# A planner in place of a hand-written order: 256-query attention, crossbar transposes and gates beside attention in a diffusion-transformer step on eight cores

## What is computed

```python
h = rms_norm(x, norm1_w) * (1 + sc1) + sh1
q, k, v, u, g = split(h @ w_in)
q, k = rms_norm(q), rms_norm(k)              # latent tokens: 2-D rotary on q and k as well
s1, s2 = softmax(q1 @ k1.T / 8), softmax(q2 @ k2.T / 8)
att = rms_norm((s1 - lam * s2) @ v) * (1 - lam_init)
sgu = gelu(u) * (w_s @ layer_norm(gelu(g)) + b_s)   # w_s: 128x128 per group, in chunks of 128 tokens
x = x + g1 * (concat(att, sgu) @ w_o)
h = rms_norm(x, norm2_w) * (1 + sc2) + sh2
x = x + g2 * (square(relu(h @ w_ff1)) @ w_ff2)
```

## Time and profile before

| what | us |
|---|---|
| median of 3 runs (2780.09 to 2781.9) | 2781.86 |
| span of the profiled execution, slowest core | 2781.8 |
| spans of the eight cores | 2769.1 to 2781.8 |
| PE busy in the span | 2514.5 (90%) |
| DVE, ACT, POOL busy | 1286.9, 751.9, 100.3 |

### The profile page before, as it was taken

One profiled execution on the slowest core, in us unless ns is written; L12 is line 12 of the kernel. 1 busy time (PEld: TensorE's weight loads), 2 busy tenths in 40 slices (PEclk: granted clock), 3 DMA queues, 4 the chain that ended last, 5 costly groups with the idle time before them and its releaser, 6 DMA issues.

```text
span 2781.8 us, 39172 instructions; the slowest of 8 cores (2769.1 to 2781.8 us)
## 1 busy us (share of the span) xinstructions
PE 2514.5 (90%) x16144; PEld 1352.3 (49%) x16144; DVE 1286.9 (46%) x2471; ACT 751.9 (27%) x1699; POOL 100.3 (4%) x162
## 2 busy tenths in 40 slices
PE   1468799899889586999999999999999999999999
PEld 0356567666666243444444444444444444444444
DVE  0257363463563222344551735528264462835537
ACT  1145455555555463422231010010100101010010
POOL 0001100000000000000000000000000000000000
PEclk9679899999999777999999999999999999999999
DMA  9962433333422637055448232222322322322336
GB/s 181 184 176 90 65 73 65 65 72 72 70 59 57 109 67 131 12 99 170 156 139 213 48 59 46 51 55 46 56 51 46 60 47 46 61 46 47 59 76 182
DMA packets 58427, 237.15 MB, mean 85 GB/s; under 512 B 20176, under 2 KB 25872, under 8 KB 35216
## 3 DMA queue, kind: packets, MB, share of 16 engines
q0 software_dynamic: 22560, 150.25, 30.7%
q1 hardware_dynamic: 35696, 84.41, 9.4%
HBM read 352.34 MB, written 32.54 MB: 138 GB/s over the span
## 4 chain that ended last, share of the span: by engine, by line
PE 82%; DMA 7%; DVE 6%; ACT 3%; issue 1%; another core or an unknown queue 1%; POOL 0%; SPq 0%; DVEq 0%; ACTq 0%
PE ps L232 81%; PE ps L240 2%; DMA sel_t<-selsum 2%; DMA xt_129<-xs 1%; DMA wr_90<-wa 1%; DMA ada_120<-wa 1%; DMA attd<-on_117 1%; DMA kr_105<-ck 1%; DVE hT L262 1%; DVE hO L262 0%; DVE a_114 L257 0%; DVE o_115 L257 0%; ACT P_108 L250 0%; DVE t_102 L257 0%
## 5 line engine op out<-in xcount | busy, mean ns | idle before, releaser
L232 PE MATMUL ps<-hT,wf_13386 128*128 128x512 bf16 x1536 | 335.6, 380 | 0.0
L232 PE MATMUL ps<-wf_13385,aT 128*128 128x512 bf16 x1536 | 334.1, 379 | 0.0
L232 PE MATMUL ps<-hT,wf_13385 128*128 128x512 bf16 x1536 | 334.1, 379 | 0.0
L232 PE MATMUL ps<-wf_13386,aT 128*128 128x512 bf16 x1536 | 334.1, 379 | 0.0
L250 ACT ACTIVATE rl_14673<-ps 128x512 f32<-128x512 f32 x96 | 57.3, 597 | 855.7 <-PE ps L232 855.7
L232 PEld LDWEIGHTS ps<-hT,wf_13386 128*128 128x128 bf16 x1536 | 150.6, 98 | 182.2 <-issue 1.9
L232 PEld LDWEIGHTS ps<-hT,wf_13385 128*128 128x128 bf16 x1536 | 150.5, 98 | 181.0
L232 PEld LDWEIGHTS ps<-wf_13386,aT 128*128 128x128 bf16 x1536 | 150.5, 98 | 181.0
L232 PEld LDWEIGHTS ps<-wf_13385,aT 128*128 128x128 bf16 x1536 | 150.0, 98 | 181.5
L257 DVE TENSOR_TENSOR aT<-rl_14674 128x512 bf16<-128x512 f32 x96 | 66.5, 692 | 264.8 <-ACT rl_14674 L250 264.8
L257 DVE TENSOR_TENSOR aT<-rl_14673 128x512 bf16<-128x512 f32 x96 | 66.5, 692 | 262.5 <-ACT rl_14673 L250 262.4
(11 more groups left out here) (663 smaller groups left out, 2898.8 us busy)
## 6 DMA issues: line engine op xcount, KB each, us to landing
wr_90<-wa POOLq DMA_DIRECT2D x32, 1024.0 KB, 8.9
wf_13386<-wf POOLq DMA_DIRECT2D x32, 1024.0 KB, 8.6
wf_13385<-wf POOLq DMA_DIRECT2D x32, 1024.0 KB, 8.7
acc<-x1d SPq DMA_DIRECT2D x12, 1024.0 KB, 42.5
ys<-acc SPq DMA_DIRECT2D x32, 256.0 KB, 2.8
ada_120<-wa POOLq DMA_DIRECT2D x3, 2048.0 KB, 28.5
ada_121<-wa POOLq DMA_DIRECT2D x3, 2048.0 KB, 38.8
wr_89<-wqkv POOLq DMA_DIRECT2D x6, 1024.0 KB, 9.6
```

Of the source, the lines that this page charges most:

```text
L232: ins = e.matmul(o, lhsT=l, rhs=r, start=st, stop=sp, skip_group_check=True)
```

## The change

The generators and the clock `S.t` go. Each piece of work is now a thread that yields the events, buffers or banks that it needs; a discrete-event model of the five engines and of two DMA rings, with a booked cost for every operation, runs all threads at planning time, and an operation is put into the program when the model's engine takes it, by the priority of its thread. What is computed stays. The other parts of the change:

- Attention works on 256 queries throughout. Four key tiles make one burst of eight score matmuls into banks 0 to 3 (two for each map), and one exponential for each map reads 1024 columns from two banks. One token stands for the score banks and one for the output banks 4 and 5; banks 6 and 7 are left to all other work.
- The transposes of Q, K, the cached keys, the attention output (on its way back from DRAM) and the second norm are transfers through the DMA crossbar, issued from SP (`turn`). The 20 input tiles are still transposed on PE; for the last 14 the modulation now reads PSUM.
- The gate matmuls run in the attention phase 3, unactivated, into SBUF; GELU and norm follow after that phase. The 32 units of `wa1` follow one another from the end of the phase-0 projections. The gate's norm weight moves into the addition after the mixing.
- The order of the projections is K, V, Q; the third weight and the tiles 6 and 7 are loaded behind the eight modulation units, the other tiles once the last of these has landed.

The core of the diff:

```diff
+PE_SWITCH = 100.0
+DMA_RATE = 335.0
+DMA_LAT = 1900.0
...
+    def dispatch(self, eng):
+        if self.busy[eng] or not self.q[eng]:
+            return
+        _, _, ev, cost, emit, lat, mode, nbytes = heapq.heappop(self.q[eng])
...
+        if mode is not None and mode != self.mode:
+            cost += PE_SWITCH
+            self.mode = mode
+        emit()
...
+    def cact(self, n, aps=0, accum=False):
+        return 100 + 0.833 * n + 93 * aps + (190 if accum else 0)
...
+    def turn(self, out, in_, key, sbuf_src=True, dr=(), prio=None):
+
+        n = count(out)
+        return self.post("sp", 300.0 + 1.7 * n, lambda: self.add(
+            "sp", lambda e: e.dma_start_transpose(out=out, in_=in_), reads=[in_] if sbuf_src else [], writes=[out], key=key, dr=dr),
+            0, nbytes=n * 256 * 2, prio=prio)
...
+        for k2 in range(8):
+            j = yield banks
+            op = S.tr([(bank16(j)[:, (c * n + i) * 128:(c * n + i + 1) * 128], xn[xnbuf[t0 + i]][:, (2 * k2 + c) * 128:(2 * k2 + c + 1) * 128])
+                       for c in range(2) for i in range(n)], identb)
+            ends.append(S.spawn(out(j, k2, op), 19))
...
-        def s5(kr):
-            j = pg.take()
-            pt = pb(j)
...
+        dst = QT[s] if kind == "q" else KT[s]
+        yield S.turn(dst[:, t0:t0 + 2].rearrange("p t h n -> p (t h) n"), kr[kj], "kr%d" % kj)
+        krs.give(kj)
...
     def attention(p):
...
+        yield (banks, range(6))
...
+        for i0 in range(0, len(items), 4):
+            its = items[i0:i0 + 4]
+            yield [KTev[p][it[2] // 2] for it in its] + [QTev[p][it[1] // 256] for it in its]
+            pj = yield Ps
+            yield Stok
...
+                    ops.append((PS[:, m * 1024 + j * 256:m * 1024 + (j + 1) * 256], KT[s][r, kt, hh, :],
+                                QT[s][r, q0 // 128:q0 // 128 + 2, hh, :], True, True))
+            yield S.mm(ops, mode="row", cost=len(its) * 112.0)
+            es = [S.act(Pt[pj][:, m, 0:n], PS[:, m * 1024:m * 1024 + n], AF.Exp, scale=0.125) for m in range(2)]
...
+    def gates():
+        yield hO_end
+        for i in range(2):
+            link(S.load(flat(wg_t[i]), wg[i], "wg%d" % i, cast=True), wg_ev[i])
+        yield [proj_end[3], att_end[2], ada_end] + wg_ev
...
+                for k0 in range(0, 16, 4):
+                    op = S.mm([(bank(j), hts(kc, tt), wg_t[nb][:, kc, :], kc == 0, kc == 15) for kc in range(k0, k0 + 4)])
+                ends.append(S.spawn(out(j, tt, nb, op), 24))
...
+    def g_norm():
+        yield [att_end[3]]
+        yield S.table(GELU_SET)
...
+            link(S.turn(att_t[j], attd[tt].rearrange("p h d -> p (h d)"), "at%d" % j, sbuf_src=False, dr=[("att", tt, h) for h in range(8)]), at_ev[tt])
...
+        yield S.turn(h2T[:, :, tt * 128:(tt + 1) * 128], xm[j], "xm%d" % j)
...
+    for p in range(1, 4):
+        S.spawn(proj(p), 30)
+    for p in range(4):
+        S.spawn(attention(p), 10)
+    S.spawn(gates(), 32)
```

More of the change, by code:

```diff
@@ L230, in fn, with run, pick, is_ps @@
+    def run(self):
+        while self.heap:
+            t, _, f = heapq.heappop(self.heap)
+            self.now = t
+            f()
+        assert self.live == 0, "threads that wait for ever: %d" % self.live
+    def pick(self, costs):
+        return min(costs, key=lambda e: max(self.until[e], self.now) + self.backlog[e] + costs[e])
+    def is_ps(self, ap):
+        return self.tens[ap.tensor.name][0] == "p"
+    def mm(self, ops, mode="full", cost=None, prio=None):
         def fn(e):
@@ new lines, in acts, with emit @@
+    def acts(self, ops, cost, table=()):
+        def emit():
+            if table:
+                self.nc.scalar.preload_act_table_set(table[0])
+            for out, in_, func, bias, scale in ops:
+                rd = [in_] + [x for x in (bias, scale) if not isinstance(x, float)]
+                self.add("act", lambda e: e.activation(out=out, in_=in_, func=func, bias=bias, scale=scale), reads=rd, writes=[out])
+            if table:
+                self.nc.scalar.preload_act_table_set(table[1])
+        return self.post("act", cost, emit, LAT["act"])
@@ L292, in wait_all_stores, with count @@
                 self.nc.sync.wait_ge(self.sems[nd.sem], nd.val)
[L295 to L319 removed]
+def count(ap):
+    return int(np.prod([n for _, n in ap.ap[1:]]))
 def bview(ap, dims):
@@ L375, in build_program, with bank, bank16 @@
     S = Sched(nc)
-    ps = [S.psum("ps%d" % j, j) for j in range(8)]
-    def pb(j):
-        return ps[j].bitcast(BF16)
+    PS = S.psum("ps")
+    PSB = PS.bitcast(BF16)
+    banks = Pool(S, range(8))
+    def bank(j):
+        return PS[:, j * 512:(j + 1) * 512]
+    def bank16(j):
+        return PSB[:, j * 1024:(j + 1) * 1024]
     o = [0]
@@ L545, in ada_cols, with evs, link, rsqrt @@
-    def ada_cols(mod, bank, n, ch, k0, which):
+    def evs(n):
+        return [Ev() for _ in range(n)]
+    def link(op, ev):
+        op.then(ev.fire)
+        return op
+    def rsqrt(out, in_, scale):
+        return S.acts([(out, in_, AF.Ln, epsc[:, 0:1], scale), (out, out, AF.Exp, 0.0, -0.5)], 480.0)
+    EARLY = 6
+    ada_ev, xev, xnev, raw_ev = evs(8), evs(20), evs(20), evs(EARLY)
+    mod_ev, h_ev = evs(4), evs(4)
+    sc_ev, ident_ev, const_ev, tab_ev, lam_ev = Ev(), Ev(), Ev(), Ev(), Ev()
@@ new lines, in attention @@
+            for e in es:
+                e.then(one)
+            todo.append((its, pj, es))
+            if not more[0].done:
+                more[0].fire()
+        yield av_end
+        yield fin
+        for j in range(6):
+            banks.give(j)
+        att_end[p].fire()
+    wg_t = [S.sbuf("wg%d" % i, [128, 16, 512], BF16, SB + (62 + 16 * i) * K) for i in range(2)]
+    raw = [S.sbuf("raw%d" % i, [128, 1024], F32, SB + (94 + 4 * ((i + 8) % 12)) * K) for i in range(12)]
+    gn = S.sbuf("gn", [128, 12, 1024], BF16, z1 - 24 * K)
@@ L1225, in build_program @@
+    S.run()
+    S.wait_all_stores([k for k in S.dlast if k[0] == "y" or k[:2] == "sk"])
     return nc
```

1684 lines of the change are left out of this document (942 added, 742 removed).

## The result

The changed kernel takes 2542.37 us (median of four runs, 2537.71 to 2549.96) against 2780.98 us: ratio 0.9144, 95% interval 0.9126 to 0.9162. Predicted were 2519 us with a range of 2450 to 2640. In some executions one die ran at a lower clock and took longer; every median and ratio here is over the others. The profiled execution of after spans 2537.7 us, 244.1 us less than that of before.

A forecast was written before the change was run, and what follows sets the result against it. The early half was taken as bound by transfers, then PE waits and score-switch gaps; the later half by matmuls. Start-up -16, phase-0 projections -30, attention -91, last phase and gates -116, second gating +6, output projection -16: -263, 2519 us, range 2450 to 2640.

The forecast's parts named there:

- The attention phases: Attention phases 0 to 2: fewer switches into and out of score matmuls cut 200 us to 173 a phase, -91 us.
- Last phase and gates: Last attention phase plus gate matmuls: waits between phases go and gates run beside attention, 155 us in all, -116 us.
- gates not beside attention: Rival for the last attention phase: planned order or late weights lose 80 of the 116 us, 2599 us; chance 0.06.
- Start-up: Loads before the last modulation matmul: one weight and three tiles moved behind it, 45.3 MB instead of 50.6, -16 us.
- Phase-0 projections: Stage after start-up: less PE, DVE and ACT work, with some 24 us for late tiles, 141.8 to 112 us, -30.
- Crossbar: Transposes moved to DMA: taken at 0.2 us a block, hidden in the output projection up to 0.27, costing nothing.
- packet price: Rival for crossbar transposes: 0.94 us a block makes the output projection 360 us instead of 168, 2711 us; chance 0.07.
- slower rival: Crossbar transposes in the output projection at 1.5 us a block, 522 us, 2873 us total, slower than before; chance 0.06.
- Starved banks: Rival for attention phases: two PSUM banks left for projections starve PE, phases stay at 200 us, 2600 us; chance 0.13.

## Why the prediction was right, and where not

**The attention phases** (-91, measured -84). The step holds: what PE loses on entering and leaving the scores falls with the number of groups. Counted in phase 1, 182 gaps of 38.5 us touch a score group before and 41 of 9.0 us after: 29.5 us less, where the sum has 32 less. The count of 77 was met by luck. The row of 49.3 us also holds gaps that touch no score group, and the prediction scaled it as a whole; after, there is one gap for each burst, and the other 15 of the 24.2 us stand elsewhere. The phases came out at 174.4 to 175.8 us, 1 to 3 above the 173, and that is luck as well: core 6 spends 28 us of them in waits for late modulation weights and rows, to which the sum gave nothing, and core 1, where these waits are 4.3 us, needs 492.5 us for all three instead of the 519 predicted. So the other terms together were too large; which of them, and what the higher granted clock gave (1.00 on core 1, 0.93 to 0.95 before), is not separated. And one number under the term was wrong. The turn "0.43 us of scores, 2 x 1.02 us and about 0.6 us of hand-over: 3.1 us" left out the 1.07 us of attention-value matmuls that PE's program puts ahead of the next scores, and a burst of eight score matmuls takes 0.61 us. At 4.18 us the loop needs 159 us a phase, close to PE's busy 158 to 170; that the sum came out well is partly luck.

**Last phase and gates** (-116, measured -134): the mechanism was right, the term mis-sized. I added PE's work to 155 us. The phase is the loop, 152.6 us from the first burst to the last, and gates and the first units of the second half (which begin at 938.0, before the last burst at 954.1) both fit into it. That 155 and 152.6 lie close is luck: one is a sum of PE's work, the other a turn times the number of bursts. The units that begin 16 us early make most of the 18 us beyond the forecast. Moved behind, the gates cost 100 us. The rival "gates not beside attention" gave 80.

**Start-up: the step that failed** (-16, measured +1.1). "The change puts one weight and three tiles behind it: 45.3 MB, so 137 us" assumed that in the kernel before all that is issued ahead of the last unit lands ahead of it. The landings show that it doesn't. Three of the nine tiles are issued on SP at 76.19, 86.26 and 102.29 us and land 82.5, 75.9 and 62.6 us later, at 158.7 to 164.9, behind the last unit, whose matmuls start at 153.20. Here is the first of them (its issue, and the times to landing of its buffer's transfers):

```profile
76.19 0.33 SPq L283 DMA_DIRECT2D xt_127<-xs  x1
...
DMA to landing us min/median/max: 5.2/7.0/82.5
```

So six tiles and three weights land ahead of that moment before, and seven tiles and two weights after; the change puts two tiles behind it, not three. Two tables of 0.5 MB, too, land at 153.3 and 155.4 us before and at 93.3 and 94.6 after. By the GB/s of the two first windows, 184 x 153.2 and 183 x 154.3 are 28.2 MB each: the changed kernel moves no less in that time. Counted by the bytes that arrive, eight units of 2.10, two weights and seven tiles of 1.05 and 1.5 of tables are 27.7 MB for after; the nine tiles and three weights counted for before would make 31. This was open to the prediction, which multiplied source bytes and never held them against the earlier trace rows. That three tiles already landed behind the last unit is shown. That the bytes set the moment is argued from these counts, with a DMA share of 0.99 and 0.96; it stays, at 153.0 and 154.7 us, where the issue behind the unit or PE's order ahead of it was changed, though the second of these edits didn't bring the earlier issues that it was made for. The named bound, 0 "if the order of landing doesn't follow the order of issue", is where it came out, and for that reason: the tile issued at 76.2 landed behind the unit issued at 114.3.

**Phase-0 projections** (-30, measured -20.6): the 24 us allowed for late tiles were short. The chain that ended last has two waits for them (start, length):

```profile
194.35 10.43 DMA xt<-xs
...
217.02 20.02 DMA xt<-xs
```

**Crossbar** (0.2 us a block taken; 0.21, 0.23 and 0.32 by three comparisons): right, and hidden, with the output projection at 166.0 us and a DMA share of 0.76. There is little to spare: the last transpose lands at 1232.3 us, 27 us behind the feed-forward's first matmul, and PE waits 1.7 us for what DVE makes of it. With 288 blocks more the stage no longer hides them. The packet price of 0.94 us and the slower rival with its 1.18 us needed packets of 117 ns and more; the added ones took 26 to 37 ns. The Trainium skill, page "Advanced Engine Details and Errata", section X-Bar Transpose (TRN2), puts a transposing DMA at some 90% of a plain one, an estimate of 0.09 us a block. The measured price is more than twice that; the conclusion, that it is hidden in this kernel, stands.

**Starved banks** (2600): phases of 174 to 176 us and no wait for banks in front of projections; the run that needs banks for K and Q as well differs by less than its interval.

Not taken out one at a time, and so read from the stages alone, are the blocks of 256 queries, the order of the projections and the transposes of the output projection.

## What to carry to other kernels

Write a software-pipelined loop down in the order in which its engine's program has it: whatever stands between one step's result and the next step's start is part of the turn, even if it is needed by neither. Then see how long the loop is without filler, and at which granted clock; work with no dependence on it, placed beside it, is nearly free up to the difference, and here it kept the clock up as well. Before a transfer is called removed, look up when it landed, and hold the sum of bytes against the window's GB/s: what lands after the moment already costs nothing ahead of it. And when a count comes out as forecast, see in the order of time whether it counts the same thing.

## What was not expected of the hardware

- The row of unexplained gaps is not the price of a switch. A single gap next to a score group is 0.21 us in the median in all three runs; the averages of the row (0.26 us before, 49.3 in 193; 0.31 after; 0.41 with bursts of two tiles, 59.9 in 145) differ because it also holds waits. In phase 1 there is a gap over 0.15 us in each of 103 steps from projections to scores before, and in none of 35 from attention-value matmuls to scores after.
- The last phase ran at a granted clock of 0.68 without gates and about 1.00 with them, and its length differed by under 2 us, by chance: the loop without gates took 4.99 us for a turn at 0.50 and 3.73 at 1.00.
- Loads of 2 KB on SP's queue landed 13 and 23 us after their issue in the changed kernel (pieces of 13.39 and 22.94 us of the chain, from 524.07 and 627.95 us on core 6).
